# Short decay levels of a gated linear recurrence as 32x32 blocks, with the sample's values spread over batches and the carried states in the weight ring

## The reference

```python
def step(S, blk):
    qb, kb, vb, ab = blk
    b = jnp.cumsum(ab, axis=2)
    diff = b[:, :, :, None, :] - b[:, :, None, :, :]
    decay = jnp.exp(jnp.where(causal, diff, -jnp.inf))
    scores = jnp.einsum('bhtd,bhsd,bhtsd->bhts', qb, kb, decay)
    o = (jnp.einsum('bhts,bhsv->bhtv', scores, vb)
         + jnp.einsum('bhtd,bhdv->bhtv', qb * jnp.exp(b), S))
    b_last = b[:, :, -1:, :]
    S = (jnp.exp(b_last[:, :, 0, :])[..., None] * S
         + jnp.einsum('bhsd,bhsv->bhdv', kb * jnp.exp(b_last - b), vb))
    return S, o
```

## Time and profile before

| what | us |
|---|---|
| median of three runs | 1896.83 |
| lowest and highest run | 1892.1, 1898.84 |
| profiled execution: time | 1899.02 |
| profiled execution: span, first to last instruction | 1897.0 |
| TensorE busy (share of the span) | 1494.9 (79%) |
| VectorE busy | 425.3 (22%) |
| ScalarE busy | 262.8 (14%) |
| GpSimd busy | 118.9 (6%) |

### The profile page before, as it was taken

One profiled execution on the slowest core, in us unless ns is written; L12 is line 12 of the kernel. 1 busy time (PEld: TensorE's weight loads), 2 busy tenths in 40 slices (PEclk: granted clock), 3 DMA queues, 4 the chain that ended last, 5 costly groups with the idle time before them and its releaser, 6 DMA issues.

```text
span 1897.0 us, 19986 instructions
## 1 busy us (share of the span) xinstructions
PE 1494.9 (79%) x8254; PEld 814.1 (43%) x8254; DVE 425.3 (22%) x931; ACT 262.8 (14%) x510; POOL 118.9 (6%) x238
## 2 busy tenths in 40 slices
PE   8998899968867776677599888999778677666773
PEld 6767466645312222122275664666453122222220
DVE  0338420151111100111410663201411111011104
ACT  1233101210000000000122321012100000000000
POOL 3113020000000000000010320200000000000000
PEclk9996799976988988888799767999869898888987
DMA  9432344863999999999923222547729999999993
GB/s 343 140 134 71 102 159 178 331 268 148 409 409 410 409 410 410 409 410 409 348 89 133 92 95 85 185 180 292 306 109 409 409 410 410 409 410 410 409 410 124
DMA packets 164424, 535.04 MB, mean 282 GB/s; under 512 B 5326, under 2 KB 22798, under 8 KB 161808
## 3 DMA queue, kind: packets, MB, share of 16 engines
q1 hardware_dynamic: 160448, 519.98, 70.8%
q0 software_dynamic: 2192, 7.98, 1.3%
q10 hardware_dynamic: 1728, 6.29, 0.9%
HBM read 521.75 MB, written 12.49 MB: 282 GB/s over the span
## 4 chain that ended last, share of the span: by engine, by line
PE 52%; DMA 25%; SPq 11%; DVE 9%; issue 1%; ACT 1%; DVEq 0%; ACTq 0%; POOL 0%
PE ps L553 12%; SPq L369 10%; DMA scr<-in_w_gate 10%; DMA W<-in_w_gate 7%; PE ps L815 7%; PE ps L798 7%; PE ps L598 6%; DMA W<-in_w_down 4%; PE ps L581 3%; PE ps L587 3%; DMA scr<-in_w_down 3%; PE ps L687 2%; PE ps L568 2%; DVE scr L1185 2%; DMA scr<-in_w_up 1%
## 5 line engine op out<-in xcount | busy, mean ns | idle before, releaser
L815 PE MATMUL ps<-W,scr 128*32 128x512 f32 x2304 | 319.9, 698 | 136.5 <-DMA W<-in_w_gate 87.0
L553 PE MATMUL ps<-XT,W 128*128 128x288 f32 x896 | 225.3, 415 | 3.0 <-ACT XT L919 2.8
L815 PEld LDWEIGHTS ps<-W,scr 128*32 128x32 f32 x2304 | 72.2, 121 | 347.2 <-issue 162.9
L553 PEld LDWEIGHTS ps<-XT,W 128*128 128x128 f32 x896 | 173.6, 195 | 53.3 <-ACT XT L919 4.1
L815 PE MATMUL ps<-scr 128*32 128x512 f32 x768 | 126.1, 792 | 86.6 <-DMA scr<-in_w_gate 37.3
L1380 DVE TENSOR_TENSOR scr<-scr,ps 128x512 f32<-128x512 f32 x16 | 11.0, 688 | 751.2 <-PE ps L815 751.2
L798 PE MATMUL ps<-scr,X 128*128 128x128 f32 (+1 forms) x864 | 171.6, 332 | 9.2 <-DVE scr L1348 9.2
L798 PEld LDWEIGHTS ps<-scr,X 128*128 128x128 f32 (+1 forms) x864 | 132.3, 208 | 67.8 <-issue 29.4
L815 PEld LDWEIGHTS ps<-scr 128*32 128x32 f32 x768 | 25.0, 132 | 175.5 <-DMA scr<-in_w_gate 55.8
L781 PE MATMUL ps<-scr 128*128 128x512 f32 x144 | 73.9, 619 | 3.9 <-ACT scr L1078 2.3
L598 PE MATMUL ps<-W,scr 128*128 128x512 f32 x128 | 60.4, 632 | 9.6 <-DVE scr L1213 9.6
(11 more groups left out here) (282 smaller groups left out, 1434.0 us busy)
## 6 DMA issues: line engine op xcount, KB each, us to landing
W<-in_w_gate SPq DMA_DIRECT2D x48, 2048.0 KB, 23.6
W<-in_w_up SPq DMA_DIRECT2D x48, 2048.0 KB, 23.8
W<-in_w_down SPq DMA_DIRECT2D x48, 2048.0 KB, 23.8
scr<-in_w_up SPq DMA_DIRECT2D x16, 2048.0 KB, 23.5
scr<-in_w_gate SPq DMA_DIRECT2D x16, 2048.0 KB, 23.6
scr<-in_w_down SPq DMA_DIRECT2D x16, 2048.0 KB, 23.9
W<-in_cache_mem_k SPq DMA_DIRECT2D x8, 2048.0 KB, 9.3
W<-in_cache_mem_v SPq DMA_DIRECT2D x8, 2048.0 KB, 8.3
```

The source lines that it names most:

```text
L553: last = mm(bank[:, 0:NT], w[:, k, c * P:(c + 1) * P], XT[:, k, :], start=(k == 0), stop=(k == KC - 1))
L815: last = mm(ps[j * CAP:(j + 1) * CAP, bank, :], x[:, k, j * CAP:(j + 1) * CAP], w[:, j, a, :], start=(k == 0), stop=(k == x.shape[1] - 1))
```

## The change

- Levels 0 to 5 never leave a block of 32 tokens, so each level and tile is scored as its four diagonal 32x32 blocks, which lie in four partition quarters of bank 0. Levels 6 and 7 are scored only where they aren't zero (six products into bank 4). One mask `cmask` of 384 columns takes the place of `masks`; the six levels are summed to `sums`, and a product with `blocks` writes them to the diagonal blocks of `st`. ACT copies the upper blocks into `st`.
- `kexp` is gone. POOL spreads the sample's values instead (`vx`), which needs no key, and the new states are two products of 512 columns (layer 1: four). Two or three of them stand ahead of `o`, the fourth behind it, in banks that the scores don't use.
- The carried states are ring units `S0` (layer 1: `S0`, `S1`), laid out on the host as partition, head, batch, value; they are updated in the slot and stored as 4 or 8 KB rows. SP's waits for the updates move to the load that follows `S0` by six.
- ACT exponentiates head h+2 after the root of head h (head 1's after the copies of head 0). POOL's exponents for head h+2 wait for the transposes of head h, and only their last two copies for its state update. DVE computes the prompt's state `sf` before `decayed`; `sf` is double.

```diff
+            carried = I[("state_hgrn", "state_gla")[l]]
+            for j in range(DVC[l]):
+                units.append((l, f"S{j}", carried[:, j * KC * HALF:(j + 1) * KC * HALF].rearrange("p (k n) -> p k n", n=HALF)))
...
-                    if n == UNIT[l, "out0"] + SLOTS:
-
+                    if n == UNIT[l, "S0"] + SLOTS:
+
+                        per = DB * DVC[l] * P
                         for h in range(HEADS):
...
                             sp.wait_ge(S("state_new"), count_at("state_new", l, h + 1))
...
+                            sp.dma_start(s_out[:, h * per:(h + 1) * per], carried_state(l, h).rearrange("p b v -> p (b v)")).then_inc(S(f"state_out{h % 2}"), 16)
...
                     if h >= 2:
-                        pool.wait_ge(S("state_new"), count_at("state_new", l, h - 1))
+                        pool.wait_ge(S("ktok_ps"), count_at("ktok_ps", l, h - 1))
...
+                    if h >= 2:
+                        pool.wait_ge(S("state_new"), count_at("state_new", l, h - 1))
                     pool.tensor_copy(dec[:, 0:PT_], bp[:, :, P - 1])
...
+                def spread_values(h):
...
+                    if h:
+                        pool.wait_ge(S("ns_ps"), count_at("ns_ps", l, 2 * DVC[l] * h))
...
+                    st.tell(tt(m["vx"][0:NS, :].rearrange("p (b v) -> p b v", b=DB),
+                               m["v"][0:NS, PT_:PT_ + 1, h * nv:(h + 1) * nv].to_broadcast([NS, DB, nv]),
+                               bmask[0:NS].unsqueeze(2).to_broadcast([NS, DB, nv]), ALU.mult), S("vx"))
...
                 exponents(0)
-                for h in range(HEADS):
+                exponents(1)
+                spread_values(0)
+                for h in range(1, HEADS):
                     if h + 1 < HEADS:
                         exponents(h + 1)
...
-                ktok_bank = 6 - l
+                ktok_bank, so_bank = (6, 3) if l == 0 else (1, 2)
+                ns_bank = (1, 2) if l == 0 else (1, 3, 2, 7)
...
-                        for lv in range(LEVELS):
-                            last = score(lv, t, ps[:, 2 * t + lv // 4, (lv % 4) * P:(lv % 4 + 1) * P])
-                        last.then_inc(S("score_ps"), 1)
+                    for lv in range(CL):
+                        for t in range(PT_):
+                            at = (lv * PT_ + t) * BLK
+                            for j in range(P // BLK):
+                                c = slice(t * P + j * BLK, t * P + (j + 1) * BLK)
+                                score(lv, c, c, ps[j * BLK:(j + 1) * BLK, 0, at:at + BLK])
+                    for lv in range(SL):
+                        at = CL * PT_ * BLK + lv * NS
+                        last = score(lv, cols(PT_), cols(PT_), ps[0:NS, 0, at:at + NS])
+                    last.then_inc(S("score_ps"), 1)
                     if h:
                         pe.wait_ge(S("ms_ready"), count_at("ms_ready", l, h))
...
+                    for t in range(PT_):
+                        at, c0 = NT + t * UPPER, t * P
+                        score(7, slice(c0, c0 + 2 * BLK), slice(c0 + 2 * BLK, c0 + P), ps[0:2 * BLK, 4, at:at + 2 * BLK])
+                        for j in range(0, P // BLK, 2):
+                            left, right = (slice(c0 + (j + i) * BLK, c0 + (j + i + 1) * BLK) for i in range(2))
+                            score(6, left, right, ps[j * BLK:(j + 1) * BLK, 4, at + 2 * BLK:at + UPPER])
...
+                    def new_part(u):
+
+                        mm(ps[:, ns_bank[u], :], m["ktok"][0:NS, PT_, :], m["vx"][0:NS, u * HALF:(u + 1) * HALF],
+                           start=True, stop=True).then_inc(S("ns_ps"), 1)
+
+                    pe.wait_ge(S("vx"), count_at("vx", l, h + 1))
+                    new_part(0)
+                    new_part(1)
+                    pe.wait_ge(S("so_ready"), count_at("so_ready", l, h + 1))
+                    if l:
+                        new_part(2)
+
+                    pe.wait_ge(S("up_ready"), count_at("up_ready", l, h + 1))
                     pe.wait_ge(S("s1_ready"), count_at("s1_ready", l, h + 1))
...
+                    if l:
+                        pe.wait_ge(S("sf_ready"), count_at("sf_ready", l, h + 1))
+                        new_part(3)
...
-                    if h + 1 < HEADS:
-                        decays(h + 1)
+
+                    act.wait_ge(S("st_ready"), count_at("st_ready", l, h + 1))
...
+                    st.tell(fn(m["st"][2 * BLK:3 * BLK, 0:PT_, 3 * BLK:P], above[2 * BLK:3 * BLK, :, 2 * BLK:UPPER], ACT.Copy), S("up_ready"))
+                    if h == 0:
+                        decays(1)
...
                     fetch_table(ACT.Exp)
+                    if h + 2 < HEADS:
+                        decays(h + 2)
...
+                    dve.wait_ge(S("score_ps"), count_at("score_ps", l, h + 1))
+                    tt(m["cs"], ps[:, 0, 0:CL * PT_ * BLK], cmask[:], ALU.mult)
...
+                    step(red(m["sums"].rearrange("p t c -> p (t c)"), m["cs"].rearrange("p (v x) -> p x v", v=CL), AX.X, ALU.add))
+                    for t in range(PT_):
+                        ins = tt(m["st"][:, t, :].rearrange("p (j c) -> p j c", c=BLK), bc(m["sums"][:, t:t + 1, :], P, P // BLK, BLK),
+                                 bc(blocks[:].unsqueeze(2), P, P // BLK, BLK), ALU.mult)
+                    tell(ins, S("st_ready"))
```

More of the change, by code:

```diff
@@ L59, in build @@
     SL = 3
+    CL = 6
+    BLK = 32
+    UPPER = 3 * BLK
     MT_ = MEM // P
@@ L153, in build @@
             if l == 0:
-                m["conv"] = [r.take(CW // P, NT) for _ in range(3)]
                 r.at = mark
                 m["up"], m["us"] = r.take(CW // P, SEQ + 2), r.take(CW // P, DB, 6)
+                m["conv"] = [r.take(CW // P, NT) for _ in range(3)]
             MIX.append(m)
@@ L319, in used @@
                     sp.wait_ge(S("mix_unit"), 2 * i + int(name[-1]) + 1)
+                elif name[0] == "S":
+                    for parity in range(2):
+                        sp.wait_ge(S(f"state_out{parity}"), count_at("state_out", l, 32 * (HEADS // 2)))
                 elif name[0] == "K":
@@ L401, in _ @@
             st.step(pool.memset(ones[:], 1.0))
-            st.step(pool.memset(masks[:], 0.0))
-            st.step(pool.affine_select(out=ident, in_=ones[:], compare_op=ALU.is_equal, fill=0.0, base=0,
+            built = scr[:, SCR_WORDS - (CL - 1) * P:].rearrange("p (v c) -> p v c", c=P)
+            st.step(pool.memset(built, 0.0))
+            st.step(pool.memset(blocks[:], 0.0))
+            st.step(pool.affine_select(out=ident[:], in_=ones[:], compare_op=ALU.is_equal, fill=0.0, base=0,
                                        pattern=[[1, P]], channel_multiplier=-1))
@@ L406, in _ @@
                                        pattern=[[1, P]], channel_multiplier=-1), S("consts"))
-            for lv in range(1, LEVELS):
+            for lv in range(1, CL):
                 B = 1 << lv
-                right = masks[:, lv, :].rearrange("p (n two h) -> p n two h", two=2, h=B // 2)[:, :, 1, :]
+                right = built[:, lv - 1, :].rearrange("p (n two h) -> p n two h", two=2, h=B // 2)[:, :, 1, :]
                 one = ones[:].rearrange("p (n two h) -> p n two h", two=2, h=B // 2)[:, :, 1, :]
@@ L624, in mixer, with score @@
                 o_bank = [5, 6]
[L625 removed]
+                ktok_bank, so_bank = (6, 3) if l == 0 else (1, 2)
+                ns_bank = (1, 2) if l == 0 else (1, 3, 2, 7)
                 for h in range(HEADS):
                     qk, kd = m["qk"][h % 2], m["kd"][h % 2]
[L629 to L632 removed]
+                    def score(lv, a, b, out):
+                        left, right = (m["k"][:, h, a], m["q"][:, h, b]) if lv == 0 else (qk[:, lv - 1, a], qk[:, lv - 1, b])
+                        return mm(out, left, right, start=True, stop=True)
@@ L1445 @@
     out["mem_k"] = _np.ascontiguousarray(out["mem_k"].transpose(0, 3, 2, 1).reshape(depth, 1, mem, mh, mhd))
+    for name in ("hgrn", "gla"):
+        _, b, h, k, v = like[f"state_{name}"]
+        out[f"{name}_s"] = _np.ascontiguousarray(out[f"{name}_s"].reshape(k, h, b, v).transpose(2, 1, 0, 3)[None])
     return tuple(out[name] for name, _ in outs)
```

169 lines of the change are left out of this document (75 added, 94 removed).

## The result

The changed kernel takes 1841.12 us (median of four runs, 1835.89 to 1844.09) against 1894.74 for the kernel before, measured beside it on the same chip: a ratio of 0.9712, 95% interval 0.968 to 0.9744. Its profiled execution took 1843.34 us with a span of 1841.6, against 1899.02 and 1897.0.

The account below looks back on a forecast made before the run. The prediction took the mixers' chain of compute steps, without transfers, as the bound. Savings of 14.0 us in layer 0 and 12.1 in layer 1, together 26.1, gave a median of 1870 us, range 1853 to 1885.

Parts of the forecast that it names:

- the expert stages only move: After the mixers: a shorter mixer moves all that follows, expert weights too; the expert stages themselves were forecast to save 0.
- the constants on GpSimd at the start: Beside the input stage, which is longer: loading the constants there was priced at nothing.
- I price the whole mixer at 1.2 GHz: TensorE in both mixers: clock stays at 0.50, so products of 128, 256, 512 columns take 0.463, 0.89, 1.78 us.
- rival 1: TensorE in the mixers: the clock rises more often; 1836 us if both mixers are fast throughout, 1853 if half; chance 0.13.
- The scores: TensorE in each mixer head: 102 records of 32x32 products take 1.8 us (bounds 1.6 and 3.1), upper scores 0.9.
- ScalarE late next: Heads 1 and 2: exponentials ahead of the key copy make ScalarE decide, 5.45 us after the squares against TensorE's 4.1.
- Head 0 behind the spread: Head 0 of each mixer waits for GpSimd's spread of the values: saves 1.0 us in layer 0, loses 0.9 in layer 1.
- Same columns for the new states: Mixers: fewer products of 512 columns keep the same columns, 3.6 us a head in layer 0 and 7.1 in layer 1.
- The order of new states and `o`: Mixers: two new-state products (layer 1: three) ahead of `o` cover mask and reduce, taken as 2.5 us, at most 3.2.
- Rival 3: Mixer scores: small products don't overlap, each record waits 110 ns for its weight load; 38 us slower, 1935; chance 0.04.
- rival 4: No difference: records issued only every 60 ns or so, or a load elsewhere takes the gain; 1891 to 1900; chance 0.05.
- SP's queue: Waits for state updates now stand ahead of `mv` loads instead of `mq`: costs nothing unless a load took over 50 us.

Follow-up runs that it names:

- before_512: The kernel before with 32 unused bytes ahead of the weight ring, so six of eight expert slots begin on multiples of 512 bytes: 1874.48 us, ratio 0.9886.
- before_spread: The kernel before, in layer 0 only, with values spread instead of keys, two products of 512 columns replacing eight of 128: 1893.05 us in one run.
- after_behind: The aligned kernel with all new-state products put behind the outputs `o` again: 1844.97 us, ratio 0.9726.
- aligned kernel: The changed kernel with the two scratch slots aligned too, so all eight expert slots begin on multiples of 512 bytes: 1837.66 us, ratio 0.9695.

## Why the prediction was wrong

**The step that failed: that the expert stages only move.** "A mixer made shorter therefore moves all that follows, the expert weights too", says the prediction, and its last paragraph of parts puts "the constants on GpSimd at the start" at "nothing". The constants were priced by their instructions; that they lie ahead of the ring in memory, and that a smaller table moves all that follows, was not seen. That is 22 us (before_512; 24.0 in the table of stages), most of the 29 by which the forecast missed. No row of the trace before could give this price; that the ring would move by 2016 bytes, and onto a multiple of 512, could be worked out from the diff.

**The term that was mis-sized: the clock.** "I price the whole mixer at 1.2 GHz." Where the clock is there, the price holds: the new states of layer 0's head 1 and of layer 1's head 1, and then those of head 2, after:

```profile
149.24:152.94 3.70, 3.70 (x8) 1.15 (x4) 3.63 (x9) 1.21 (x5) 3.69 (x9) 0.50 0.00 0
1052.01:1057.42 5.41, 5.41 (x7) 1.83 (x7) 5.30 (x19) 1.43 (x5) 2.62 (x6) 0.50 0.00 0
1076.70:1079.80 3.10, 3.10 (x7) 1.24 (x7) 3.06 (x16) 1.43 (x5) 0.00 (x0) 0.90 0.00 0
```

3.70 and 5.41 us were forecast as 3.6 and 5.34; the last takes 3.10, at 0.90. By heads the forecast saved 1.0, 3.9, 3.9, 5.2 and -0.9, 4.5, 4.5, 4.0. Measured, from the reciprocals: 0.5, 4.3, 3.5, 7.3 and -0.1, 4.8, 7.5, 6.9. Of the excess of 8.7 us, 8.0 lie in the last head of layer 0 (clock 0.71) and the last two of layer 1 (0.68 and 0.63). Their new states alone gave 5.5 of it: 1.91 us at 1.00, 3.10 at 0.90 and 3.77 at 0.71, where 3.6, 5.34 and 5.34 were forecast. Over both mixers the clock was 0.63 and 0.65, not "near 0.5". This is rival 1 in part, put at 0.13. Its argument against, that the clock stood at 0.50 in "just the stretches that remain", took a clock that belonged to one sequence of instructions for a property of the instructions.

**What held, step by step.**
- The scores: 98 records between 157.96 and 159.37 above, 1.41 us, so 14.4 ns each and 1.5 for the 102, where 1.8 was taken and 1.6 was the lower bound. Scores and upper scores together took 3.06 us, forecast 2.7; so the upper ones were priced too low, 0.9 for 1.6. The Trainium skill, "TensorE: Matmul & The Clock Gate", section "Wait — 56ns, not 53.3ns?", has a least distance of about 25 ns between starts; this row, of products that rotate over four column groups, disagrees, and the measurement decides.
- ScalarE late next: TensorE waits 2.17 and 1.65 us for the key copies of heads 1 and 2 in layer 0, where 1.35 was priced. The chain of waits passes there through ScalarE.
- Head 0 behind the spread: its first new-state product waits 3.16 us for GpSimd in layer 0 and 4.02 in layer 1, and the net result, 0.5 and -0.1 us, lies near the forecast of 1.0 and -0.9.
- Same columns for the new states: before_spread.
- The order of new states and `o`: worth some 6 us by after_behind, and for another reason than given: what it covers is ScalarE's copies, which the prediction put beside the path with mask and reduce.
- Rival 3 (the small products don't overlap) is out by the first point, rival 4 (no difference) by the result. SP's queue added no wait to the chain in the mixers.

The small loss of 3.4 us in the rest of the span was not followed up, and its cause stays open. 2.5 us are lost between layer 1's mixer and its experts, where the granted clock is 0.50 for the first 5.8 us, and 2.1 ahead of that mixer; 1.9 are gained ahead of layer 0's.

## What to carry to other kernels

When a change alters the size of any buffer, work out what moves behind it, and look at the start of each buffer that transfers fill, before taking an untouched stage as unchanged. A kernel that is limited by its loads should place those buffers on 256-byte boundaries on purpose; here a pad of 32 bytes was enough. Price TensorE's columns at both levels of the clock and let the range hold both, and where products of few rows fill a stretch, try them with zero rows added.

## What the runs showed that I had not expected

- The rate of these loads into on-chip memory depends on where they begin: 409 to 410 GB/s at 32, 64, 128 or 224 bytes past a multiple of 256, 421 to 422 on one. With 4 KB rows that is 2.9%, and 22 us of this kernel.
- Products of 32 columns that rotate over four column groups start 14.4 ns apart at the low clock. In head 0, at the full clock, the first 98 records lie between 125.52 and 126.41, 9.1 ns apart.
- Multiplying zeros made the kernel faster: four times the rows for the same columns raised the clock of the mixers' heads 1 to 3 from 0.53 to 0.74 (aligned kernel) up to 0.75 to 0.90, and took 22 us off. In the kernel before, where another engine releases `o`, the same gave 8.
